# Output weights of two mixers taken two units at a time, and squares of four norms added up on GpSimd

## The reference

```python
def rms_norm(x, g):
    xf = x.astype(jnp.float32)
    y = xf * lax.rsqrt(jnp.mean(xf * xf, axis=-1, keepdims=True) + EPS)
    return (y * g.astype(jnp.float32)).astype(x.dtype)

def first_block(...):
    for i in range(DEPTH):
        ...
        h = rms_norm(x, norm_mix[i]) * (1 + scale1) + shift1
        ...                      # i == 0: mla_mixer, i == 1: dilated_mixer, both end in  o @ w_o
        x = x + gate1 * y
        h = rms_norm(x, norm_mlp[i]) * (1 + scale2) + shift2
        x = x + gate2 * (jnp.square(jax.nn.relu(h @ mlp_w1[i])) @ mlp_w2[i])

def second_block(...):
        hn = _rmsnorm(x, norm_mix[l])
        z = hn @ w_in[l]
        ...
        y = jnp.concatenate([_rmsnorm(y_a, norm_grp_a[l]), _rmsnorm(y_b, norm_grp_b[l])], axis=-1)
        x = x + y @ w_out[l]
        x = x + _memory_cross_attention(_rmsnorm(x, norm_cross[l]), _rmsnorm(mem, norm_mem[l]),
                                        w_q_mem[l], w_kv_mem[l], w_o_mem[l])
        x = x + _peer(_rmsnorm(x, norm_ffn[l]), w_query[l], sub_keys[l], expert_u[l], expert_v[l])
    return _rmsnorm(x, norm_final)
```

## Time and profile before

| | us |
|---|---|
| median of 3 runs | 2017.81 (2015.99 to 2019.18) |
| profiled execution | 2018.96 |
| its span | 2017.2 |
| TensorE busy | 1966.6 |
| VectorE busy | 1410.9 |
| ScalarE busy | 1143.8 |
| GpSimd busy | 311.6 |

### The profile page before, as it was taken

One profiled execution on the slowest core, in us unless ns is written; L12 is line 12 of the kernel. 1 busy time (PEld: TensorE's weight loads), 2 busy tenths in 40 slices (PEclk: granted clock), 3 DMA queues, 4 the chain that ended last, 5 costly groups with the idle time before them and its releaser, 6 DMA issues.

```text
span 2017.2 us, 34914 instructions
## 1 busy us (share of the span) xinstructions
PE 1966.6 (97%) x14224; PEld 1824.1 (90%) x14224; DVE 1410.9 (70%) x2546; ACT 1143.8 (57%) x1935; POOL 311.6 (15%) x333
## 2 busy tenths in 40 slices
PE   8998999999999989999999999999999999999997
PEld 5798999999888879999989999999999998888886
DVE  6777765887776667656756478999986765555554
ACT  5865543556667545544755464457677754444444
POOL 0010000000000000001100000038868940000000
PEclk9999999999999999999999999999999999999999
DMA  9465787346444327666435355554444445555553
GB/s 358 158 209 179 245 285 245 120 141 238 155 151 142 116 89 239 196 178 230 136 114 166 123 169 172 179 177 147 157 148 156 139 156 189 189 189 190 189 190 117
DMA packets 97743, 356.25 MB, mean 177 GB/s; under 512 B 11104, under 2 KB 11232, under 8 KB 97200
## 3 DMA queue, kind: packets, MB, share of 16 engines
q1 hardware_dynamic: 84240, 305.04, 45.3%
q0 software_dynamic: 12624, 48.08, 7.3%
q10 hardware_dynamic: 720, 0.91, 0.1%
HBM read 352.94 MB, written 1.05 MB: 175 GB/s over the span
## 4 chain that ended last, share of the span: by engine, by line
PE 90%; DVE 4%; ACT 3%; DMA 2%; issue 1%; SPq 1%; DVEq 0%; ACTq 0%; POOLq 0%
PE psum L589 24%; PE psum L591 24%; PE psum L590 24%; PE psum L582 17%; PE psum L596 2%; DVE wl L2088 1%; DMA first<-in_ada_w 1%; SPq L3099 1%; ACT work L1409 1%; ACT wh L1421 0%; DMA araw<-in_ada_w 0%; ACT na L1409 0%; DMA memx<-in_mem 0%; DMA raw<-in_mla_w_kvb 0%; DVE xc L2068 0%
## 5 line engine op out<-in xcount | busy, mean ns | idle before, releaser
L2088 DVE TENSOR_TENSOR wl<-raw,wh 128x1024 fp32r<-128x1024 f32 (+1 forms) x566 | 689.8, 1222 | 410.8 <-ACT wh L1421 409.4
L1421 ACT ACTIVATE wh<-raw 128x1024 fp32r<-128x1024 f32 (+1 forms) x566 | 593.7, 1050 | 429.1 <-PE psum L591 390.4
L589 PE MATMUL psum<-peer_hh,wh 128*128 128x256 f32 x1024 | 296.3, 289 | 0.0
L590 PE MATMUL psum<-peer_hl,wh 128*128 128x256 f32 x1024 | 290.3, 284 | 0.0
L591 PE MATMUL psum<-peer_hh,wl 128*128 128x256 f32 x1024 | 290.3, 283 | 0.0
L590 PE MATMUL psum<-wl,csh 128*128 128x512 f32 x512 | 201.9, 394 | 0.0
L589 PE MATMUL psum<-wh,csh 128*128 128x512 f32 x512 | 201.8, 394 | 0.0
L591 PE MATMUL psum<-wh,csl 128*128 128x512 f32 x512 | 201.8, 394 | 0.0
L589 PEld LDWEIGHTS psum<-peer_hh,wh 128*128 128x128 f32 x1024 | 194.5, 190 | 0.0
L590 PEld LDWEIGHTS psum<-peer_hl,wh 128*128 128x128 f32 x1024 | 194.3, 190 | 0.0
L591 PEld LDWEIGHTS psum<-peer_hh,wl 128*128 128x128 f32 x1024 | 194.3, 190 | 0.0
(11 more groups left out here) (453 smaller groups left out, 4861.3 us busy)
## 6 DMA issues: line engine op xcount, KB each, us to landing
raw<-in_mlp_w SPq DMA_DIRECT2D x128, 512.0 KB, 4.2
raw<-in_eu SPq DMA_DIRECT2D x128, 512.0 KB, 3.4
raw<-in_ev SPq DMA_DIRECT2D x128, 512.0 KB, 3.4
araw<-in_ada_w POOLq DMA_DIRECT2D x76, 512.0 KB, 4.7
raw<-in_dil_qk SPq DMA_DIRECT2D x48, 512.0 KB, 4.0
raw<-in_dil_v SPq DMA_DIRECT2D x24, 512.0 KB, 3.5
raw<-in_w_in SPq DMA_DIRECT2D x16, 512.0 KB, 3.5
raw<-in_w_query SPq DMA_DIRECT2D x16, 512.0 KB, 3.5
```

The lines of the kernel that those rows point to most:

```text
L589: e.matmul(o, l[0], r[0], start=start, stop=False, skip_group_check=loose)
L590: e.matmul(o, l[0], r[1], start=False, stop=False, skip_group_check=loose)
L1421: e.activation(b.wh[v % NSPLIT][:, 0:cols], b.raw[v % NRAW][:, 0:cols], ACT.Copy).then_inc(S.hi, 1)
L2088: e.tensor_tensor(b.wl[v % NSPLIT][:, 0:cols], b.raw[v % NRAW][:, 0:cols], b.wh[v % NSPLIT][:, 0:cols].bitcast(F32), ALU.subtract).then_in ...
```

## The change

**Pairs at the ends of the mixers.** `rows_end` now also does the last two units of `mla_o` and `dil_o`, with one square sum inside (after tile 5), a second when the eighth tile is done, and the last two behind it. In `mla_order` units 0 to 5 stand at attention steps 13, 14, 15, 16, 17 and 19, and 6 and 7 behind all steps. The conversion that goes with unit 7 moves on ScalarE ahead of the fourth square and on DVE behind the residuals. On `mo` `rows_end` has no sums now.

**Squares on GpSimd.** In both MLPs GpSimd adds the squares of tiles 0 to 6 into the buffer `sb2` (`add_tiles`), and TensorE does two multiplications at the end (`tile_sums`); ScalarE's later squares wait for an addition instead of a matmul. In MLP 0 the additions stand among GpSimd's transfers of `araw`; in MLP 1 behind all of them. For ya and yb GpSimd adds the two halves of the squares (128x512), and TensorE does two sums instead of four each. For out2 and mo the squares go to four buffers of 512 (`pairs`), GpSimd adds them up (`add_pairs`), and TensorE does one multiplication (`pair_sums`) instead of eight. For out2 it stands behind w_mem_v 7, not 4; for mo behind query 3. The root and the columns of both move later (columns of mo: behind query 4, not 2), and the squares of mo move to the first two queries.

**Low parts.** For mo ScalarE computes x times gain for the odd tiles (`cross_odd`), GpSimd makes their low parts (mix_hl), DVE those of the even tiles. GpSimd's transfer of `skT` stands behind this and the additions of mo.

```diff
@@ mla_order, cross_order and the experts' order
-    outer = {12: 0, 13: 1, 14: 2, 15: 3, 16: 4, 17: 5, 18: 6, 19: 7}
+    outer = {13: 0, 14: 1, 15: 2, 16: 3, 17: 4, 19: 5}
...
-    return out
+    return out + [("hi", 6), ("lo", 6), ("wo", 6), ("wo", 7)]
...
-    out = [("unit", "w_mem_v", 4), ("tiles", None, 0), ("total", None, None), ("unit", "w_mem_v", 5),
-           ("tiles", None, 4), ("unit", "w_mem_v", 6), ("root", None, None), ("unit", "w_mem_v", 7)]
+    out = [("unit", "w_mem_v", 4), ("tiles", None, 0), ("unit", "w_mem_v", 5),
+           ("tiles", None, 4), ("unit", "w_mem_v", 6), ("unit", "w_mem_v", 7), ("total", None, None)]
     for i in range(8):
         out.append(("unit", "w_q_mem_2", i))
         if i == 0:
+            out.append(("root", None, None))
+        if i == 1:
             out.append(("columns", None, None))
...
         out.append(("query", c, None))
-        if c == 0:
+        if c == 3:
             out += [("root", None, None)]
-        if c == 2:
+        if c == 4:
             out.append(("columns", None, None))
@@ TensorE
-        for k in range(nk):
-            pe.wait_ge(S.act, at[tag, "sq", int(k >= nk // 2)])
-            mm(ps[:, 0:256], ones, q3[:, k, :], k == 0, k == nk - 1, mark=(tag, "sum") if k == nk - 1 else None)
+        pe.wait_ge(S.pool, at[tag, "added"])
+        for k in range(nk // 2):
+            mm(ps[:, 0:256], ones, q3[:, k, :], k == 0, k == nk // 2 - 1, mark=(tag, "sum") if k else None)
...
+    def tile_sums(tag, m):
+
+        ps = take(tag, "total")
+        pe.wait_ge(S.pool, at[tag, "added", 6])
+        mm(ps[:, 0:256], ones, m.sbf[:, 0:256], True, False)
+        pe.wait_ge(S.act, at[tag, "square", 7])
+        mm(ps[:, 0:256], ones, m.rbf[:, 768:1024], False, True, mark=(tag, "squares", 7))
+        give(tag, "total", sem=S.act, key=(tag, "ms"))
+
+    def pair_sums(tag, pairs):
+
+        ps = take(tag, "total")
+        pe.wait_ge(S.pool, at[tag, "added", 3])
+        mm(ps[:, 0:256], ones, pairs[0][:, 0:256], True, True, mark=(tag, "squares", 3))
...
-            if c in (5, 7):
+            if ring is not None and c in (5, 7):
                 square_sums(tag, c // 2 - 2, ring)
         for c2 in range(4):
             give(tag, c2, sem=S.dve, key=(tag, "out", c2))
+        if ring is not None:
+            square_sums(tag, 2, ring)
+            square_sums(tag, 3, ring)
...
+                if i < 6:
+                    pe.wait_ge(S.dve, at["mla", "out", i])
+                    rows_unit("mla_o", "mla_w_o", i, sp(m.hh, i), i == 0, False)
+                elif i == 7:
+                    pe.wait_ge(S.dve, at["mla", "out", 7])
+                    rows_end("mla_o", "mla_w_o", 6, [sp(m.hh, 6), sp(m.hh, 7)], m.ring)
...
+            elif i == 6:
+                pe.wait_ge(S.dve, at["dil", "out", 7])
+                rows_end("dil_o", "dil_w_o", 6, x, m.work)
@@ ScalarE
         if k >= 4:
-            ac.wait_ge(S.pe, at[tag, "squares", k - 4])
+            ac.wait_ge(S.pool, at[tag, "added", max(1, k - 4)])
...
         for c2 in range(4):
+            if c2 == 3:
+                unit("mla_w_o", 7)
             square("mla_o", c2, m.ring, ("mla_o", "out", c2))
...
-            for k in (2 * c2, 2 * c2 + 1):
+            ac.wait_ge(S.dve, at["mo", "out", c2])
+            act(m.odd[:, c2 * 256:c2 * 256 + 256], b.xs3[:, 2 * c2 + 1, :], ACT.Copy,
+                scale=vc(b, "ffn", 2 * c2 + 1), mark=("odd", c2))
+            for k in (2 * c2 + 1, 2 * c2):
                 tile_high("n6 gain", ("mo", "out", c2), k, vc(b, "ffn", k), x.hh)
-            square("mo", c2, m.ring, ("mo", "out", c2))
@@ VectorE
-        rows_residual("mla_o", u, lambda c: b.mod[:, 16 + c:17 + c])
+        rows_residual("mla_o", u + 1, lambda c: b.mod[:, 16 + c:17 + c])
+        unit("mla_w_o", 7)
@@ GpSimd
+    def add_tiles(tag, m, every=0):
+
+        total = m.sbf[:, 0:256]
+        for k in range(1, 7):
+            if every:
+                tick(8 if k == 1 else 4, every)
+            po.wait_ge(S.act, at[tag, "square", k])
+            own()
+            tt(total, m.rbf[:, (k % 4) * 256:(k % 4) * 256 + 256], total if k > 1 else m.rbf[:, 0:256], ALU.add,
+               (tag, "added", k))
+
+    def add_pairs(tag, pairs):
+
+        for c2 in range(1, 4):
+            po.wait_ge(S.act, at[tag, "square", c2])
+            own()
+            tt(pairs[0], pairs[0], pairs[c2], ALU.add, (tag, "added", c2))
+        own()
+        tt(pairs[0][:, 0:256], pairs[0][:, 0:256], pairs[0][:, 256:512], ALU.add, (tag, "added", 3))
...
+        for name, sq in (("ya", m.xcf), ("yb", m.work)):
+            po.wait_ge(S.act, at[name, "sq", 1])
+            tt(sq[:, 0:512], sq[:, 0:512], sq[:, 512:1024], ALU.add, (name, "added"))
...
-    tick(64, 2)
+    tick(36, 2)
+    add_tiles(("mlp0", 2), b.mlp[0], 2)
```

More of the change, by code:

```diff
@@ L490, in buffers @@
     m.tmp = sb("cross_tmp", 768, where=s)
-    m.ring = sb("cross_ring", 1024, where=s)
+    m.ring = sb("cross_ring", 2048, where=s)
+    m.odd = sb("cross_odd", 1024, where=s)
+    m.pairs = [m.ring[:, z:z + 512] for z in range(0, 2048, 512)]
     m.qM = sb("qM", 2048, where=s).rearrange("p (k t) -> p k t", k=8)
@@ L1179, in rows @@
         def rows(i):
[L1180 to L1195 removed]
+            x = [[m.o[:, k, 0, :], m.o[:, k, 1, :]] for k in (i, min(i + 1, 7))]
+            if i < 6:
+                pe.wait_ge(S.dve, at["dil", "out", i])
+                rows_unit("dil_o", "dil_w_o", i, x[0], i == 0, False)
+            elif i == 6:
+                pe.wait_ge(S.dve, at["dil", "out", 7])
+                rows_end("dil_o", "dil_w_o", 6, x, m.work)
         for kind, i, z in DIL_ORDER:
@@ L1219, in dilated @@
                 rows(i)
-        for c2 in range(4):
-            give("dil_o", c2, sem=S.dve, key=("dil_o", "out", c2))
-            square_sums("dil_o", c2, m.work)
     def mixer2():
@@ L1311, in cross @@
             if kind == "total":
-                for c2 in range(4):
-                    square_sums("out2", c2, x.xcf)
+                pair_sums("out2", x.pairs)
             elif kind == "step":
@@ L1911, in mixer2 @@
         for c2 in range(4):
-            square("out2", c2, m.xcf, ("out2", "out", c2))
+            square("out2", c2, m.pairs, ("out2", "out", c2), True)
     def mem_values(c2, u):
@@ L3081, in pool_program @@
         pass
+    add_tiles(("mlp1", 2), b.mlp[1])
     mixer2()
-    phase("cross")
+    phase("cross", lambda: add_pairs("out2", b.mix.pairs))
     peer()
```

97 lines of the change are left out of this document (43 added, 54 removed).

## The result

The changed kernel took 2003.78 us (median of 4 runs, 2003.09 to 2007.03), the kernel before 2017.26 us (median of 4): a ratio of 0.9936, 95% interval 0.9918 to 0.9953. The forecast was 2003.0 us. In the profiled execution the span fell by 15.8 us, from 2017.2 to 2001.4.

A forecast was written before the change was run, and what follows sets the result against it. The prediction took TensorE, busy 97% of the span, as the bound. Terms 6.1 + 1.7 + 2.0 + 1.8 + 1.4 + 1.8 = 14.8 us, off the median 2017.81, gave 2003.0 us; range 1997.7 to 2009.5.

The forecast's parts named there:

- MLP 0 and MLP 1: Second products: seven of eight sums leave TensorE in each, 3.0 us each, 6.1 together; range 5.2 to 6.5.
- ya and yb: Group norms: 8 sums become 4, the added GpSimd additions costing TensorE nothing; 1.7 us, range 0 to 1.7.
- out2: Norm ahead of cross attention: 3.0 us of sums less 1.0 for slowed DVE; gain 2.0, range 1.0 to 3.0.
- mo: Norm ahead of the experts: 2.8 us gained, less 1.0 for the later skT transfer; gain 1.8, range 0 to 3.0.
- end of the MLA mixer: Last two units paired: fourth square 9.0 us after the start, not 11.1, less 0.7; gain 1.4, range 0 to 2.0.
- end of the dilated mixer: Same pairing with the last head already done: 734.8 against 736.6; gain 1.8 us, range 1.0 to 2.2.
- The price of a sum: One square sum removed from TensorE's chain saves 0.433 us, from sums standing alone there (0.43 to 0.46).
- rival C: No change: the sums filled time in which TensorE would have waited for wl or wh anyway; 2017.8 us, chance 0.05.
- The 5.1 us: Ahead of cross attention: DVE's loss by the Trainium skill's full-block rule, making the whole 2007.1 us.
- Rival B: Last pair gives nothing in either mixer, starting only when the last head is done; 3.2 us less, 2006.2, chance 0.12.
- Rival D: Slower: araw transfers queue behind MLP 0's additions, six at some 3.5 us each, +21; 2024 us, chance 0.03.
- The half clock (E): Short stretches at 1.2 GHz, mostly after idling; one more or less is 1.7 to 3.5 us; no chance of its own.

The follow-up runs named there:

- e5: Changed kernel with four araw transfers in MLP 0 moved from ahead of GpSimd's first addition to behind the sixth; 2007.94 us, ratio 0.9945.
- e9: Changed kernel with GpSimd issuing the skT transfer ahead of its four additions for the norm before the experts; 2005.71 us, ratio 0.9941.
- e6: Changed kernel with eight unread constant multiplications on TensorE in each of the three 3.7 us gaps between stages; 2004.05 us, ratio 0.9932.
- e8: Changed kernel with skT issued first, root's table loaded before the first square at both mixer ends, and four TensorE gaps filled; 1998.73 us, ratio 0.9907.
- e1: Changed kernel with only the MLPs' square sums put back on TensorE, one for each tile; 2009.02 us, ratio 0.9958.

## Why the prediction was right

| term | forecast | measured by undoing it |
|---|---|---|
| MLP 0 and MLP 1 | 3.0 + 3.0 | 3.03 + 3.03 |
| ya and yb | 0.87 + 0.87 | 0.36 + 0.85 |
| out2 | 2.0 | 1.71 |
| mo | 1.8 | 2.40 (0.50 when skT lands late) |
| end of the MLA mixer | 1.4 | 1.16 (0.8 to 1.25 by execution) |
| end of the dilated mixer | 1.8 | 1.82 |
| sum | 14.8 | 14.4 |

- **The price of a sum** was taken from the chain and not from the mean of the records, and it held wherever sums stood in a stream that nothing else bounded: 3.03 us for seven, twice. It also held that the extra multiplications hide behind the last square and the mixer's waits.
- **ya was mis-sized.** The step that said that the group norms give their full 1.7 looked at whether TensorE waits for the squares and not at what it waits for next. It stood at wl 15 us later, and half of the time won was spent there. This is rival C in small, at one place of eight.
- **out2 was right for its reason.** The sum, 3.0 less 1.0 for a slowed DVE, stands against 3.2 less 1.46. DVE lost 1.8 us and TensorE 1.46, where the prediction put 1.0; where the other 0.2 came from was not looked into. The prediction's reading of the earlier trace rows, a loss and not a full stop, was wrong: those rows add up two instructions each. Taken singly, the two k took 1.61 and 1.71 us instead of 0.77, and each had begun 1.0 and 1.1 us before the end of one of DVE's operations; the two wl took 1.76 and 1.75 instead of 1.22 and had begun 0.7 us before the end of a k. Each waited for nearly the whole rest. The 5.1 us took all additions for one long hold, and they are not.
- **mo had two errors.** The new waits were put at 1.8 and are 1.75, but the sums were worth 2.75 instead of 3.03 and a new wait of 0.15 for wl came in, so 2.40 stands against the 2.8 without the transfer; and the late transfer was put at 1.0 in every execution. Its row was a single transfer (7.7 us); with the additions first eight took 5.4 to 9.5 us, so the cost is none in most executions and 1.7 to 1.9 in some (two of the eight traces in which the additions stand first).
- **The ends of the mixers.** The fourth square came 9.1 us after the pair's start, as stepped through (9.0), and the pair started 0.9 us later than unit 6 would (0.7). Rival B, that the MLA pair starts as late as unit 7 did, fell: it started at 148.46, not 152.55.
- **Rival D** had the mechanism right (DVE waits for araw) and the price wrong by a factor of more than ten, since it allowed for one unit of lead and there are two.
- **The half clock (E)** was priced at half of its length. Against the run with fills, at the start of an MLP a stretch of 4 us cost 0.2 to 0.5 us and one of 7 us 0.7 to 1.7; at 362 us, in the dilated mixer's stream, one of 4 us cost 1.1 to 1.4, and near 92 and 984 us 1.3 to 1.5.
- **One of its signs of being wrong came.** It named a wait for wl of more than 1 us at w_mem_v 6 or 7, and 1.08 us stand ahead of w_mem_v 7. It was the disturbance that the term for out2 had priced, too low by 0.5 us, and not the failure of the sum. The other two signs stayed away: skT was waited for at most 1.9 us, and DVE never waited for araw in MLP 0 until e5 forced it.
- **Luck.** That the median came within 1 us of the forecast owes something to errors that cancel: ya 0.5, out2 0.3 and the MLA mixer 0.2 too high, mo 0.6 too low. The median of the changed kernel itself moved by more than that from series to series (2003.78, 2006.03 and 2005.33).

The span fell by 15.8 us where the parts add up to 14.4. The difference lies in the two executions and not in the edits: the kernel before had slow stretches near 92 and 990 us (1.3 and 1.5 us), which the changed kernel's first trace had not, while that trace's stretches at the MLPs' starts were longer (0.7 and 1.0 us), and the kernel before waited some 0.6 us more in the first part of the second block's mixer, as e9 did, which has the changed kernel's instructions there. With these the parts come to 16.1 us, 0.3 more than the span.

## What to carry to other kernels

Price a removed instruction by the chain, then ask what the engine would stand at next; where it runs in a stream without waits the full price comes back, and where TensorE waits for another engine a few units further on, part of it is lost there. Work moved to GpSimd is paid by DVE where both read two inputs from the on-chip memory: count what is left of the other engine's instruction each time one begins, and put the work where nobody waits for DVE. With runs that scatter by more than the terms, undo one part at a time and compare stretches between fixed instructions; a total would not have told these terms apart.

## What the runs showed of the hardware

- **Gaps of 3.0 to 3.7 us on TensorE bring the lower clock**, in all twelve traces without fills, at the four places where they stand: the granted clock fell to 0.50 in the gap or within 1 us behind it. Filling them with multiplications that nobody reads kept the clock at 1.00 there (e6, e8). In some executions stretches also begin elsewhere (near 92, 362 and 984 us); two of the three traces that had one at 362 us had fills. TensorE had stood for 1.5 us ahead of the place near 92 us and for 1.8 us ahead of that near 984 us in all fourteen traces, and the clock fell at each in four of them. What decides it stays open.
- **TensorE has two paces at the same granted clock**: 118.7 and 120.0 ns from matmul to matmul (592 and 585 in 70 us). One MLP runs wholly or partly at one of them; of fourteen traces MLP 0 was at the slower in three, in one of them not to its end, and MLP 1 in two (e9, and e1 in part). It makes 2.3 us in MLP 0 alone. The cause is open; no run was made for it.
- **DVE and GpSimd stop each other instruction by instruction** where both have two inputs in the on-chip memory: one that begins while the other's is under way takes longer by what is left of that, less 0.13 to 0.20 us (mix_hl 1.51 instead of 0.48 us, an addition of 128x512 2.09 instead of 1.28). A DVE operation with one input in PSUM (xT<-psum,xT at 1073.21 us) took 0.42 us beside an addition, as it does alone. Which of the two goes first can turn round: in MLP 0 an addition (0.75 us at 303.09) began 0.35 us behind a wl and lost nothing, and the wl took 2.19 us instead of 1.22.
